# Routing to experts with unscaled transposes, token parts on VectorE, and the raw weight buffers at the top of SBUF

## The chip, the cores and the metric

The kernel runs on one core of a Trainium2 chip. The metric is device time in microseconds (us) for one execution. Five engines take part, each with its own instruction queue: the matrix engine (TensorE, in the profile PE, with PEld for its weight loads), VectorE (DVE), ScalarE (ACT), GpSimd (POOL) and SyncE (SP), which issues most transfers. They meet only at semaphores.

## The reference, cut to what matters

The program computes two transformer blocks on 256 tokens of width 1024. The first has a gated recurrence beside latent attention, cross-attention to a memory and a convolved feed-forward. The second has dilated and differential attention, a feed-forward, a gated recurrence in chunks (`hgrn`), and last a mixture of eight experts, of which each token uses two:

```
u = rms_norm(x, moe_norm)                 # x / rms(x) * gain, by token
logits = u @ w_router                     # 256 x 8
top_vals, top_idx = top_k(logits, 2)
top_w = softmax(top_vals)                 # over the two
gates = sum(one_hot(top_idx) * top_w)
for e in range(8):
    y = (silu(u @ w_gate[e]) * (u @ w_up[e])) @ w_down[e]
    out = out + gates[:, e:e+1] * y
x = x + out
```

All is fp32. The expert width is 3584. The row factor 1/rms(x) is one number for each token, so the logits of a token can be scaled by it after the product as well as before.

## The kernel before

**Weights.** All weights lie in memory as 458 pieces of 1 MB, called units (128 partitions x 2048 fp32); with three loaded again behind the last expert there are 461 loads. SyncE loads unit n into one of seven buffers of `raw`. ScalarE rounds it into one of three buffers of `wh` (`hi_to`, L1401, and `hi` in the expert loop, L2011), the high part. VectorE subtracts that from `raw` into `wl` (`lo_to`, L2087, and `lo`, L2990), the low part. The matrix engine makes each product from three: high x high, low x high, high x low (`split_product`, L421, L423, L430). A raw buffer is free for the next load when the low part is made; a `wh` buffer is free for the unit three later when its products are done. Units 0 to 121 (`N_FIXED` is 122) belong to everything ahead of the experts, and units 122 on to the experts, 42 each. The first three of the experts, 122 to 124, are prepared before the expert loop.

**Order.** The order of work on each engine is written out by hand. `hi_to(m)` and `lo_to(m)` say at which place in an engine's list units up to m are prepared. `step` makes VectorE wait for its own last operation.

**Normalisation.** There are two orders of it. For the names in `SCALED_LATER` the matrix engine transposes `x` as it is (L454), ScalarE and VectorE make high and low parts of the turned tiles with the gain (`norm_high`, L1434; `norm_low`, L2127), and the row factor comes in later. For the others, `moe_norm_2` among them, ScalarE squares both tiles (L1421), VectorE works out the factors and scales the rows into `xn` (L2103 to L2118), and then `xn` is transposed (L467). `residual` (L2150) adds the last projection's four PSUM banks to `x`.

**Routing, the seam.** After `residual` and the normalisation, the matrix engine makes the logits (8 x 256), VectorE copies them (L2912), the matrix engine turns them to token rows (L1211), and VectorE ranks them by comparing all pairs. L2918 and L2919 compare, L2922 multiplies ties by a fixed mask, one tile each, L2923 to L2925 add, reduce and compare with 2. Ten small matmuls (L441) count each token's slot in its expert, L2931 to L2938 turn that into slots, and `choose` (L2945) makes a 0/1 matrix `G` for the first expert.

Beside it, the tokens are split exactly into three bf16 parts, so that a matmul with `G` gathers them exactly. GpSimd multiplies the normalised rows by the gain (L2059, after the gain's transfer, L2055), ScalarE copies to bf16 (L1999, part 0), GpSimd subtracts (L2063), ScalarE copies (part 1), and VectorE subtracts into part 2 (L2952). The gather (L1234) has two runs of 24 matmuls, q = 0 for columns 0 to 511 and q = 1 for the others, and starts when all parts are there. ScalarE copies each run's bank (L2003) and VectorE subtracts (L2962); then the first expert's matmuls start. VectorE meanwhile clears `GT`, `yh` and `yl` (L2954 to L2957) and works out the two weights from an exponential (L2041; L2968 to L2983).

**Experts.** Fori loops on all engines, 42 units each, in chunks of 512 hidden columns. In the first chunk the matrix engine also scatters the previous expert's result (`scatter`, L1306 and L1307, which read `GT`, `yh` and `yl`), between the second and the third unit. For the first expert these hold zeros.

## Time and profile before

| what | before |
|---|---|
| median of 3 runs | 1944.0 us (1942.25 to 1947.37) |
| profiled execution, its own time | 1941.3 us |
| its span, first to last instruction | 1939.4 us |
| TensorE matmul busy | 1854.3 us (96%) |
| VectorE busy | 1552.2 us (80%) |
| ScalarE busy | 1255.3 us (65%) |
| GpSimd busy | 11.3 us (1%) |
| mean granted TensorE clock | 0.981 of 2.4 GHz |
| read from memory | 488.75 MB, 253 GB/s over the span |

The durations below come from the profiled execution, the comparison from the medians. A line such as L430 is a line of the kernel; a helper's line serves many callers. The granted clock is 1.00 at 2.4 GHz and 0.50 at 1.2 GHz. Idle time of an engine matters only where the chain that ended last runs through it.

### The profile page before, as it was taken

The page shows a single profiled execution, that of the slowest core. Times are in us where ns is not written, and L with a number is a line of the kernel's source. Part 1 is how long each engine was busy: PE and PEld are TensorE (multiplying, and loading weights), DVE is VectorE, ACT ScalarE, POOL GpSimd, SP SyncE. Part 2 cuts the span into 40 slices and gives each one's busy share as a digit, 9 for nine tenths or more (in the row PEclk, how much of TensorE's full clock was granted, in tenths as well). Part 3 has the DMA queues.
Part 4 walks back from the last instruction along what each step waited for, and adds up shares of the span by engine and source line. Part 5 has one row for each costly group of instructions (what it writes and reads, how often), then busy time and mean ns, then how long its engine had stood idle before and what let it go on. Part 6 is the DMA issues. An engine that isn't in the chain of part 4 may idle for free.

```text
span 1939.4 us, 27547 instructions
## 1 busy us (share of the span) xinstructions
PE 1854.3 (96%) x10240; PEld 1580.6 (82%) x10240; DVE 1552.2 (80%) x1589; ACT 1255.3 (65%) x1290; POOL 11.3 (1%) x9
## 2 busy tenths in 40 slices
PE   7888999998899999998799999999999999999997
PEld 7777999877799988876688888888888888888886
DVE  8966788476567645665898998989989899899997
ACT  6966565356554435554577777777777777777775
POOL 0000000000000000001000000000000000000000
PEclk9999999999799999999899999999999999999999
DMA  9422455542145554332499998999989989899894
GB/s 366 146 88 91 170 180 190 192 153 92 64 159 189 176 193 152 131 130 98 172 368 356 343 376 335 373 361 344 381 325 367 381 336 371 337 367 380 327 368 194
DMA packets 68330, 490.85 MB, mean 253 GB/s; under 512 B 7713, under 2 KB 8097, under 8 KB 8993
## 3 DMA queue, kind: packets, MB, share of 16 engines
q1 hardware_dynamic: 67968, 488.52, 67.1%
q0 software_dynamic: 288, 1.31, 0.2%
q8 instruction: 51, 0.84, 0.2%
q14 instruction: 23, 0.18, 0.0%
HBM read 488.75 MB, written 1.05 MB: 253 GB/s over the span
## 4 chain that ended last, share of the span: by engine, by line
PE 87%; DVE 6%; ACT 5%; issue 2%; DMA 0%; SPq 0%; ACTq 0%; DVEq 0%
PE ps L421 26%; PE ps L423 20%; PE ps L430 20%; PE ps L432 6%; PE ps L425 6%; DVE wl L2087 1%; PE ps L441 1%; PE ps L1322 1%; ACT wh L1401 1%; PE ps L1234 1%; PE ps L1053 1%; PE ps L467 1%; PE ps L1090 1%; PE ps L826 1%; PE ps L827 1%
## 5 line engine op out<-in xcount | busy, mean ns | idle before, releaser
L2990 DVE TENSOR_TENSOR wl<-raw,wh 128x2048 fp32r<-128x2048 f32 x336 | 761.1, 2288 | 63.3 <-ACT wh L2011 59.8
L2011 ACT ACTIVATE wh<-raw 128x2048 fp32r<-128x2048 f32 x336 | 642.1, 1918 | 180.9 <-PE ps L430 180.8
L421 PE MATMUL ps<-wh,hTh 128*128 128x512 f32 (+2 forms) x1128 | 443.2, 394 | 7.1 <-DVE hTl L2375 1.7
L2087 DVE TENSOR_TENSOR wl<-raw,wh 128x2048 fp32r<-128x2048 f32 x125 | 286.0, 2290 | 128.5 <-ACT wh L1401 127.9
L423 PE MATMUL ps<-wh,hTh 128*128 128x512 f32 x896 | 349.3, 390 | 0.0
L1401 ACT ACTIVATE wh<-raw 128x2048 fp32r<-128x2048 f32 x125 | 238.6, 1913 | 140.9 <-PE ps L430 73.2
L430 PE MATMUL ps<-wl,hTh 128*128 128x512 f32 (+2 forms) x1128 | 301.1, 386 | 0.0
L423 PE MATMUL ps<-wh,hTl 128*128 128x512 f32 (+2 forms) x680 | 260.4, 385 | 0.0
L421 PEld LDWEIGHTS ps<-wh,hTh 128*128 128x128 f32 x1128 | 212.2, 188 | 50.1 <-issue 5.4
L430 PEld LDWEIGHTS ps<-wl,hTh 128*128 128x128 f32 x1128 | 210.1, 188 | 42.8
L421 PE MATMUL ps<-hTh,wh 128*128 128x256 f32 x896 | 223.2, 286 | 2.5 <-DVE hTl L2127 2.3
L425 PE MATMUL ps<-hTl,wh 128*128 128x256 f32 x896 | 221.1, 284 | 0.0
L423 PEld LDWEIGHTS ps<-wh,hTh 128*128 128x128 f32 x896 | 168.4, 188 | 33.8
L421 PE MATMUL ps<-wh,hTl 128*128 128x512 f32 x448 | 176.9, 395 | 2.9 <-DVE hTl L2995 2.4
L421 PEld LDWEIGHTS ps<-hTh,wh 128*128 128x128 f32 x896 | 172.9, 193 | 4.9 <-issue 3.1
L425 PEld LDWEIGHTS ps<-hTl,wh 128*128 128x128 f32 x896 | 172.9, 193 | 0.1
L423 PEld LDWEIGHTS ps<-wh,hTl 128*128 128x128 f32 x680 | 128.2, 188 | 23.3
L430 PE MATMUL ps<-wl,hTl 128*128 128x512 f32 x448 | 138.1, 389 | 0.0
L432 PE MATMUL ps<-hTh,wl 128*128 128x256 f32 x896 | 125.7, 283 | 0.0
L432 PEld LDWEIGHTS ps<-hTh,wl 128*128 128x128 f32 x896 | 115.6, 192 | 0.0
L421 PEld LDWEIGHTS ps<-wh,hTl 128*128 128x128 f32 x448 | 84.1, 188 | 24.2 <-issue 7.5
L430 PEld LDWEIGHTS ps<-wl,hTl 128*128 128x128 f32 x448 | 84.1, 188 | 17.8
(433 smaller groups left out, 2026.4 us busy)
## 6 DMA issues: line engine op xcount, KB each, us to landing
raw<-in_units SPq DMA_DIRECT2D x461, 1024.0 KB, 6.9
x<-in_x SPq DMA_DIRECT2D x2, 512.0 KB, 5.4
work<-in_lru_w SPq DMA_DIRECT2D x1, 1024.0 KB, 15.4
xn<-in_mem SPq DMA_DIRECT2D x1, 1024.0 KB, 17.5
out<-x SPq DMA_DIRECT2D x2, 512.0 KB, 3.4
consts<-in_consts POOLq DMA_DIRECT2D x1, 768.0 KB, 4.6
work<-in_moe_gain POOLq DMA_DIRECT2D x1, 512.0 KB, 3.8
consts<-in_consts SPq DMA_DIRECT2D x1, 352.0 KB, 11.5
```

Source lines behind the costliest of these rows:

```text
L421: nc.tensor.matmul(out, sh, mh, start=(first and j == 0), stop=False)
L423: nc.tensor.matmul(out, sl, mh, start=False, stop=False)
L425: nc.tensor.matmul(out, sh, ml, start=False, stop=False)
L430: ins = nc.tensor.matmul(out, sh, ml, start=False, stop=done)
L432: ins = nc.tensor.matmul(out, sl, mh, start=False, stop=done)
L441: ins = nc.tensor.matmul(out, l, r, start=(first and j == 0), stop=(last and j == len(pairs) - 1))
L467: ins = nc.tensor.transpose(ps[:, NORM_BANK[name] + g, c2 * S + t * P:c2 * S + (t + 1) * P], rows_of(name)[:, t, c * P:(c + 1) * P], ident)
L826: nc.tensor.matmul(out, hTh[:, k, ts], hi[:, o], start=first, stop=False, skip_group_check=u == 2)
L1401: A(wh[:, n % SPLIT, :], raw[:, n % RAW, :], ACT.Copy).then_inc(sem("hi_made"), 1)
L2011: A(wh[:, n % SPLIT, :], raw[:, n % RAW, :], ACT.Copy).then_inc(sem("hi_made"), 1)
L2087: V.tensor_tensor(wl[:, n % SPLIT, :], raw[:, n % RAW, :], wh[:, n % SPLIT, :].bitcast(F32), ALU.subtract).then_inc(sem("lo_made"), 1)
L2990: V.tensor_tensor(wl[:, n % SPLIT, :], raw[:, n % RAW, :], wh[:, n % SPLIT, :].bitcast(F32), ALU.subtract).then_inc(sem("lo_made"), 1)
```

## The change

Four things are edited. The seven raw buffers move from the lowest addresses to above the work area, padded to a multiple of 128 bytes, and `work` and `junk` move with them; number and sizes are as before. `moe_norm_2` joins `SCALED_LATER`: `x` is turned unscaled, and the factor is applied to the logits when they are copied from PSUM. The tokens are scaled and split on VectorE, in halves of 512 columns (`tokens_half`, `tokens_rest`), with ScalarE's bf16 copies in halves between them (`token_part`), and GpSimd computes nothing. The second gather run waits for the second halves alone (`TOKEN_STEPS`). The two softmax weights come from two sigmoids in place of an exponential, an add, a reciprocal and a product. With them several things change place: the low part of unit 123 goes between the first two residual adds, that of unit 124 and the memsets go behind the gathered tokens' low parts, and the gain's transfer is issued once the previous mixer's outputs are turned, into `xn`, which is free then.

```diff
-    raw = sb("raw", [RAW, UNIT])
...
     xn = sb("xn", [TT, D])
-    junk = sb("junk", [HALF])
+    work_at = nc.sbuf_base
+    work = sb("work", [WORK])
     consts_at = nc.sbuf_base
     consts = sb("consts", [N_CONST])
     cols = sb("cols", [N_COLS])
     rows = sb("rows", [N_ROWS])
     pos = sb("pos", [TT], I32)
+    junk = sb("junk", [HALF])
     small = sb("small", [416])
-    work_at = nc.sbuf_base
-    work = sb("work", [WORK])
+    sb("pad", [(-nc.sbuf_base % 128) // 4])
+    raw = sb("raw", [RAW, UNIT])
 
...
-    moe_gain = area(4096, D)
+    moe_gain = xn[:, 0, :]
...
+    TOKEN_STEPS = (4, 6)
...
-    NORM_BANK = {n: 4 if n in ("hgrn_norm_2", "ffn_norm_2") else 0 for n in NORMS}
-    SCALED_LATER = ("mem_attn_norm", "attn_norm_2", "ffn_norm_2")
+    NORM_BANK = {n: 4 if n in ("hgrn_norm_2", "ffn_norm_2", "moe_norm_2") else 0 for n in NORMS}
+    SCALED_LATER = ("mem_attn_norm", "attn_norm_2", "ffn_norm_2", "moe_norm_2")
...
-        return area(0, TT, D) if name == "mem_attn_norm" else xn
+        return {"mem_attn_norm": area(0, TT, D), "moe_norm_2": area(10240, TT, D)}.get(name, xn)
...
-    rtv = {k: tiny(2) for k in ("v1", "v2", "ex", "w1", "w2")}
+    rtv = {k: tiny(2) for k in ("v1", "v2", "w1", "w2")}
...
         norm("moe_norm_2")
         pe.wait_ge(sem("router_lo"), 1)
-        split_product(ps[0:NE, 7, 0:S], [(rh[:, k * NE:(k + 1) * NE], rl[:, k * NE:(k + 1) * NE], hTh[:, k, :], hTl[:, k, :])
-                                         for k in range(KD)], ready=tile_ready, rest=lambda: None).then_inc(sem("logits"), 1)
+        for k in range(KD):
+            w = slice(k * NE, (k + 1) * NE)
+            tile_ready(k)
+            nc.tensor.matmul(ps[0:NE, 0, 0:S], rh[:, w], hTh[:, k, :], start=(k == 0), stop=False)
+            nc.tensor.matmul(ps[0:NE, 0, 0:S], rl[:, w], hTh[:, k, :], start=False, stop=False)
+            ins = nc.tensor.matmul(ps[0:NE, 0, 0:S], rh[:, w], hTl[:, k, :], start=False, stop=(k == KD - 1))
+        ins.then_inc(sem("logits"), 1)
         pe.wait_ge(sem("logits_read"), 1)
         for t in range(TT):
-            ins = nc.tensor.transpose(ps[:, 6, t * NE:(t + 1) * NE], logitsT[:, t * P:(t + 1) * P], ident[0:NE, 0:NE])
+            ins = nc.tensor.transpose(ps[:, 1, t * NE:(t + 1) * NE], logitsT[:, t * P:(t + 1) * P], ident[0:NE, 0:NE])
         ins.then_inc(sem("logits"), 1)
 
...
-                pe.wait_ge(sem("tokens_left"), 3)
+                pe.wait_ge(sem("tokens_left"), TOKEN_STEPS[q])
...
-        norm("moe_norm_2", N_FIXED + SPLIT)
-        for i in range(2):
-            act.wait_ge(sem("tokens_left"), i + 1)
-            A(parts[i][:], tokens[:], ACT.Copy).then_inc(sem("tokens_part"), 1)
+        A(warm, ones[:, 0:1], ACT.Sqrt)
+        norm_stats("moe_norm_2", (0,), False)
+        norm_high("moe_norm_2", 0)
+        norm_stats("moe_norm_2", (1,))
+
+        def token_part(i, h, left):
+
+            act.wait_ge(sem("tokens_left"), left)
+            cs = slice(h * HALF, (h + 1) * HALF)
+            A(parts[i][:, :, cs], tokens[:, :, cs], ACT.Copy).then_inc(sem("tokens_part"), 1)
+
+        token_part(0, 0, 1)
+        hi_to(N_FIXED + SPLIT)
+        token_part(1, 0, 2)
+        token_part(0, 1, 3)
+        token_part(1, 1, 5)
+        act.wait_ge(*reached("route_diff", 1))
+        A(rtv["w1"], rtv["v2"], ACT.Sigmoid, scale=-1.0)
+        A(rtv["w2"], rtv["v2"], ACT.Sigmoid).then_inc(sem("route_exp"), 1)
+
...
-        act.wait_ge(*reached("route_diff", 1))
-        A(rtv["ex"], rtv["v2"], ACT.Exp).then_inc(sem("route_exp"), 1)
...
-        pool.wait_ge(*reached("x_ready", X_AFTER["hgrn"]))
+        pool.wait_ge(*reached("hgrn_oT_ps", 4))
         pool.dma_start(moe_gain, moe_gain_d.partition_broadcast(P)).then_inc(sem("moe_gain"), 16)
-        pool.wait_ge(*reached("norm_xn", TT * len(NORMS)))
-        pool.wait_ge(sem("moe_gain"), 16)
-        for t in range(TT):
-            ins = G_.tensor_tensor(tokens[:, t, :], xn[:, t, :], moe_gain, ALU.mult)
-        ins.then_inc(sem("tokens_left"), 1)
-        pool.wait_ge(sem("tokens_part"), 1)
-        pool.wait_ge(sem("tokens_left"), 1)
-        G_.tensor_tensor(tokens[:], tokens[:], parts[0][:], ALU.subtract).then_inc(sem("tokens_left"), 1)
...
-        def residual(stage, n, following, bank=4):
+        def residual(stage, n, following, bank=4, then=0):
 
             lo_to(following + 1)
             for t in range(TT):
                 for h in range(2):
+                    if 2 * t + h == 1:
+                        lo_to(then)
...
-        residual("hgrn_x_change", 7, N_FIXED, 0)
-
-
-        norm("moe_norm_2", N_FIXED + SPLIT - 1)
+        residual("hgrn_x_change", 7, N_FIXED, 0, N_FIXED + 2)
+
+
+        norm_low("moe_norm_2", 0)
+        norm_rows("moe_norm_2")
+        token_scale = rstd[:, 2 * NORM_OF["moe_norm_2"]:2 * NORM_OF["moe_norm_2"] + TT]
+        dve.wait_ge(*reached("norm_xn", TT * len(NORMS)))
+        dve.wait_ge(sem("moe_gain"), 16)
+
+        def tokens_half(t, h):
+            cs = slice(h * HALF, (h + 1) * HALF)
+            return V.scalar_tensor_tensor(out=tokens[:, t, cs], in0=x[:, t, cs], scalar=token_scale[:, t:t + 1], in1=moe_gain[:, cs],
+                                          op0=ALU.mult, op1=ALU.mult)
+
+        def tokens_rest(i, h, part):
+
+            dve.wait_ge(sem("tokens_part"), part)
+            cs = slice(h * HALF, (h + 1) * HALF)
+            V.tensor_tensor((tokens, parts[2])[i][:, :, cs], tokens[:, :, cs], parts[i][:, :, cs],
+                            ALU.subtract).then_inc(sem("tokens_left"), 1)
+
         dve.wait_ge(sem("logits"), 1)
-        V.tensor_copy(logitsT, ps[0:NE, 7, 0:S]).then_inc(sem("logits_read"), 1)
+        V.tensor_copy(logitsT, ps[0:NE, 0, 0:S]).then_inc(sem("logits_read"), 1)
+        tokens_half(0, 0)
+        tokens_half(1, 0).then_inc(sem("tokens_left"), 1)
         L, rank, s1, s2, tmp = (rt[:, i] for i in range(5))
         dve.wait_ge(sem("logits"), 2)
-        step(V.tensor_copy(L, ps[:, 6, 0:TT * NE].rearrange("p (t e) -> p t e", t=TT)))
+        for t in range(TT):
+            ins = V.tensor_scalar(L[:, t, :], ps[:, 1, t * NE:(t + 1) * NE], token_scale[:, t:t + 1], None, ALU.mult)
+        step(ins)
...
-        lo_to(N_FIXED + SPLIT)
+        tokens_rest(0, 0, 1)
+        tokens_half(0, 1)
+        tokens_half(1, 1).then_inc(sem("tokens_left"), 1)
...
         choose(0)
-        dve.wait_ge(sem("tokens_part"), 2)
-        V.tensor_tensor(parts[2][:], tokens[:], parts[1][:], ALU.subtract).then_inc(sem("tokens_left"), 1)
-        dve.wait_ge(sem("tokens_left"), 3)
-        V.memset(GT.bitcast(F32), 0.0)
-        V.memset(gates[:, 0, :], 0.0)
-        V.memset(yh.bitcast(F32), 0.0).then_inc(sem("y_lo"), 1)
-        V.memset(yl.bitcast(F32), 0.0).then_inc(sem("y_lo"), 1)
-
...
-
-
+        tokens_rest(1, 0, 2)
+        tokens_rest(0, 1, 3)
         s1 = xsel
         for s, r, v in ((s1, 0.0, "v1"), (s2, 1.0, "v2")):
             step(V.tensor_scalar(s, rank, r, None, ALU.is_equal))
             step(V.tensor_tensor(tmp, s, L, ALU.mult))
             step(V.tensor_reduce(rtv[v], tmp, AX, ALU.add))
         V.tensor_tensor(rtv["v2"], rtv["v2"], rtv["v1"], ALU.subtract).then_inc(sem("route_diff"), 1)
+        tokens_rest(1, 1, 4)
+
...
+
+
         for q in range(2):
             tokens_low(q, 0)
+        lo_to(N_FIXED + SPLIT)
+        V.memset(GT.bitcast(F32), 0.0)
+        V.memset(gates[:, 0, :], 0.0)
+        V.memset(yh.bitcast(F32), 0.0).then_inc(sem("y_lo"), 1)
+        V.memset(yl.bitcast(F32), 0.0).then_inc(sem("y_lo"), 1)
         dve.wait_ge(*reached("route_exp", 1))
-        step(V.tensor_scalar(rtv["w1"], rtv["ex"], 1.0, None, ALU.add))
-        step(V.reciprocal(rtv["w1"], rtv["w1"]))
-        step(V.tensor_tensor(rtv["w2"], rtv["w1"], rtv["ex"], ALU.mult))
         for t in range(TT):
             step(V.tensor_scalar(tmp[:, t, :], s1[:, t, :], rtv["w1"][:, t:t + 1], None, ALU.mult))
             step(V.scalar_tensor_tensor(out=gates[:, 1:NE + 1, t], in0=s2[:, t, :], scalar=rtv["w2"][:, t:t + 1], in1=tmp[:, t, :],
```

## Rows read from the trace of the kernel before

**Rows 1.** The page, part 4: shares of the chain that ended last, by engine.
```profile
PE 87%; DVE 6%; ACT 5%; issue 2%; DMA 0%; SPq 0%; ACTq 0%; DVEq 0%
```

**Rows 2.** Windows by stage, under their own column heads.
```profile
core 0: us, PE busy (x) PEld busy (x) DVE busy (x) ACT busy (x) POOL busy (x), PEclk, DMA share, GB/s
907.00:939.00 32.00, 15.07 (x102) 13.08 (x100) 24.57 (x49) 12.45 (x17) 10.38 (x4) 0.68 0.23 83
...
1056.69:1179.97 123.28, 122.91 (x591) 101.58 (x591) 113.49 (x75) 91.85 (x64) 0.00 (x0) 1.00 0.94 358
```

**Rows 3.** Page part 5, the expert stage's high parts; waits of SyncE's queue (us, times, longest).
```profile
L2011 ACT ACTIVATE wh<-raw 128x2048 fp32r<-128x2048 f32 x336 | 642.1, 1918 | 180.9 <-PE ps L430 180.8
...
SPq L1345 <- DVE wl L2990: 781.5, 329, 18.0
```

**Rows 4.** Chain of waits through the seam: start us, us, what.
```profile
906.80 0.47 PE ps L430 x2
...
911.31 3.68 PE ps L467 x16
...
917.61 0.94 PE ps L430 x8
...
920.22 3.99 DVE work L2922
...
924.24 0.24 DVE work L2922
...
925.48 2.29 DVE wl L2087
...
930.06 2.21 DVE work_b L2952
...
932.41 5.02 PE ps L1234 x48
...
939.01 0.49 PE ps L421
```

**Rows 5.** Timeline at the `attn_norm_2` normalisation: start us, us, engine, line, what.
```profile
547.29 1.91 PE L454 MATMUL ps<-consts,x 128*128 128x128 f32 x16
...
549.45 3.23 DVE L2127 SCALAR_TENSOR_TENSOR hTl<-ps,cols,hTh 128x256 fp32r<-128x256 f32 x8 [1.27 <-ACT hTh L1434]
...
552.48 1.11 ACT L1421 ACTIVATE xn<-x 128x1024 f32<-128x1024 f32 x1
```

**Rows 6.** Page part 6 (KB, us to landing), then the seam's timeline.
```profile
work<-in_moe_gain POOLq DMA_DIRECT2D x1, 512.0 KB, 3.8
...
918.08 1.91 ACT L1999 ACTIVATE work_b<-work 128x2048 bf16<-128x2048 f32 x1 [0.41 <-POOL work L2059]
...
920.07 4.05 POOL L2063 TENSOR_TENSOR work<-work,work_b 128x2048 f32<-128x2048 f32 x1 [2.02 <-ACT work_b L1999]
...
938.07 1.28 ACT L2041 ACT_TABLE_LOAD   x1
```

**Rows 7.** Timeline of VectorE around the last residual adds and before.
```profile
891.19 1.23 DVE L2807 TENSOR_TENSOR xn<-xn,work 128x1024 f32<-128x1024 f32 x1
...
904.57 0.69 DVE L2150 TENSOR_TENSOR x<-ps,x 128x512 f32<-128x512 f32 x1 [0.67 <-PE ps L430]
...
909.84 1.42 DVE L2118 TENSOR_SCALAR xn<-x,small 128x1024 f32<-128x1024 f32 x2
```

**Rows 8.** Timeline of VectorE at the first expert's start.
```profile
934.73 0.11 DVE L2968 TENSOR_SCALAR work<-junk 128x16 f32<-128x16 f32 x1
...
941.26 0.38 DVE L2983 COPY junk<-junk 128x8 f32<-128x8 f32 x2
...
944.01 2.29 DVE L2990 TENSOR_TENSOR wl<-raw,wh 128x2048 fp32r<-128x2048 f32 x1 [2.37 <-ACT wh L2011]
```

**Rows 9.** Windows of 1 us through the seam, columns as in rows 2.
```profile
916.00:917.00 1.00, 1.00 (x9) 0.65 (x7) 0.77 (x2) 1.00 (x1) 1.00 (x1) 0.74 1.00 426
...
936.00:937.00 1.00, 1.00 (x12) 1.00 (x11) 0.67 (x2) 0.00 (x0) 0.00 (x0) 0.50 0.00 0
```

More of the change, by code:

```diff
@@ L2950, in _ @@
         choose(0)
-        dve.wait_ge(sem("tokens_part"), 2)
-        V.tensor_tensor(parts[2][:], tokens[:], parts[1][:], ALU.subtract).then_inc(sem("tokens_left"), 1)
-        dve.wait_ge(sem("tokens_left"), 3)
-        V.memset(GT.bitcast(F32), 0.0)
-        V.memset(gates[:, 0, :], 0.0)
-        V.memset(yh.bitcast(F32), 0.0).then_inc(sem("y_lo"), 1)
-        V.memset(yl.bitcast(F32), 0.0).then_inc(sem("y_lo"), 1)
-        def tokens_low(q, e):
-            dve.wait_ge(sem("tokens_hi"), e * 2 + q + 1)
-            V.tensor_tensor(xel[:, 4 * q:4 * q + 4, :], ps[:, TOKEN_BANKS[q], :].rearrange("p (a b) -> p a b", a=4),
-                            xeh[:, 4 * q:4 * q + 4, :].bitcast(F32), ALU.subtract).then_inc(sem("bank7_free"), 1)
+        tokens_rest(1, 0, 2)
+        tokens_rest(0, 1, 3)
         s1 = xsel
@@ L2971, in _, with tokens_low @@
         V.tensor_tensor(rtv["v2"], rtv["v2"], rtv["v1"], ALU.subtract).then_inc(sem("route_diff"), 1)
+        tokens_rest(1, 1, 4)
+        def tokens_low(q, e):
+            dve.wait_ge(sem("tokens_hi"), e * 2 + q + 1)
+            V.tensor_tensor(xel[:, 4 * q:4 * q + 4, :], ps[:, TOKEN_BANKS[q], :].rearrange("p (a b) -> p a b", a=4),
+                            xeh[:, 4 * q:4 * q + 4, :].bitcast(F32), ALU.subtract).then_inc(sem("bank7_free"), 1)
         for q in range(2):
             tokens_low(q, 0)
+        lo_to(N_FIXED + SPLIT)
[3 more added lines that the diff above has]
+        V.memset(yl.bitcast(F32), 0.0).then_inc(sem("y_lo"), 1)
         dve.wait_ge(*reached("route_exp", 1))
-        step(V.tensor_scalar(rtv["w1"], rtv["ex"], 1.0, None, ALU.add))
-        step(V.reciprocal(rtv["w1"], rtv["w1"]))
-        step(V.tensor_tensor(rtv["w2"], rtv["w1"], rtv["ex"], ALU.mult))
         for t in range(TT):
```

## The prediction

> **What bounds the kernel now.** I read the page first. The matrix engine carries 87% of the chain that ended last; VectorE has 6% of it, ScalarE 5% [rows 1]. That is an average over stages, so next come the windows by stage: the routing seam from 907 to 939 us, and the second expert [rows 2]. In an expert the matrix engine is busy for all but 0.4 us of 123.28 us; in the seam for 15 of 32 us. The feeding engines confirm it: of ScalarE's 180.9 us idle ahead of the 336 unit copies, the matrix engine ended 180.8, no transfer any, and SyncE's queue waits 781 us for buffers that VectorE frees [rows 3]. Nothing in the change touches an expert's matmuls. Hence an edit is worth what it takes from or adds to the time between the last projection matmul and the first expert matmul; whatever is left over then shifts the end one for one.
>
> The chain of waits through the seam [rows 4]: the last projection ends at 906.80 + 0.47 = 907.27, and the first expert matmul starts at 939.01. That is 31.7 us. Its marks are the end of the router product (917.61 + 0.94, logits read at 918.57), the gather's start (932.41) and its end (937.43). So there are three stretches: 11.3 us, 13.8 us and 6.6 us.
>
> **Stretch 1, to the logits.** Before, both tiles are summed and scaled before the transposes begin. Now `x` is transposed unscaled, the row factor is applied to the logits. The same order is in the trace for `attn_norm_2`: transposes start as the projection ends, at 547.29, and VectorE's eight low parts run from 549.45 to 552.68 [rows 5]. So 552.68 - 547.27 = 5.4 us from the last projection to the last low part. Then six router matmuls for the last pair of tiles, 0.12 us each at full clock as their 0.94 us for 8 show [rows 4], and a step of about 0.15: 6.3 us. Row statistics end earlier: the last square starts 552.48 - 547.27 = 5.2 us after the projections and takes 1.1 [rows 5], then come three tiny operations of 0.2. The saving is 11.3 - 6.3 = 5.0 us.
>
> The lower part of unit 123 (2.29 us [rows 4]) moves between the first and second residual add. Its cover is the projection still running, which lets an add start each 0.69 + 0.67 = 1.36 us [rows 7]. It makes the second add late (906.2 for 904.57), but the last three adds need 0.7 each and finish near 908.2; the transpose that needs the last one is thirteenth, at about 908.6. Without the cover it would cost up to 0.3. The gain vector's transfer moves forward, behind the turned outputs of the previous mixer; POOL's queue holds nothing else then, and it lands in 3.8 us [rows 6], more than 10 us before use.
>
> **Stretch 2, to the gather.** Start from 13.84 us and go in VectorE's order.
> - The tie product took 3.99 us once and 0.24 us for its twin [rows 4]. It ran beside GpSimd's subtraction of 4.05 us, from 920.07 to 924.12 [rows 6], and ended at 924.21. GpSimd now computes nothing: -3.75.
> - Two token halves before the logits are used, 128x512 with two inputs. VectorE's rows are 1.23 for 128x1024 with two inputs [rows 7] and 0.69 for 128x512 [rows 7]; back to back, 1.3 for two. They cover the wait for the small transposes, about 0.35: +0.95. Second scaling of the logits: +0.1.
> - Unit 124's low part leaves: -2.29.
> - The first remainder half comes in, +1.2, with two more token halves, +1.25. They cover the ten slot matmuls, which took no longer than unit 124's 2.29 us, since VectorE went on at its end (927.77) without a wait.
> - The last remainder before the gather shrinks from 2.21 us [rows 4] to a half, 1.2: -1.0.
> The sum is -3.75 + 0.95 + 0.1 - 2.29 + 1.2 + 1.25 - 1.0 = -3.55 us.
>
> ScalarE's copies to bf16 are now halves, about 1.06 each from 1.91 for the whole [rows 6]. The first ends about 1 us after the first two token halves, under VectorE's comparisons. Unit 124's high part (1.9 us) follows it, then each copy is ready before VectorE reaches its subtraction. If one were late, VectorE would stop for at most 1 us, and the slot steps, the routing of units and the gather queue behind it.
>
> For the token half no row has this operation with both inputs in SBUF. From below, the scaling of rows moves 128x1024 in 0.71 us [rows 7], so 0.36 a half; from above, 0.69. I take the upper, as two-input rows are all at that pace; four halves at the lower would give 1.3 us more.
> The Trainium skill (VectorE: DVE Perf Modes, "Mode 2×_2P — use both read ports for one tensor") says fp32 reaches two elements a cycle only with one tensor source. By it a two-source product runs at the slower pace, and the sum stays; were it wrong here, the sum would be 8.6 us.
>
> **Stretch 3, gather to expert.** The gather takes 5.02 us for 48 matmuls, then 1.6 us of copy, subtraction and start [rows 4]. Now the first half needs only the first halves of the parts. The second half waits for VectorE: a remainder (1.15), seven small routing steps (1.35 at the 0.2 us each that the ten slot operations and their handovers show between 927.77 and 930.06 [rows 4]), a second remainder (1.15), 0.1 of start. That is 3.75 us after the first start, where 24 matmuls take 2.5: +1.25 us. ScalarE's sigmoids, with a table load of 1.28 as its exponential had [rows 6], end before the second half does; the copy of the first half they delay is not the last thing needed. Their cover is gather work; uncovered they cost 1.7.
>
> Sum: 5.0 + 3.55 - 1.25 = 7.3 us less.
>
> **After the start.** Before, VectorE was free for the loop 2.6 us after the first expert matmul and then idle 2.37 us, so its first low part began at +5.0 [rows 8]. Now unit 124's low part (2.3), the memsets (2.3, from the gather's start to the first routing step at 934.73) and the gates (1.5, seven steps) stand behind the start: +6.0. The matrix engine needs unit 124's low part at +7.3 (two units of twelve matmuls and eight more, at the 0.23 that 0.47 for two gives [rows 4]) and has it at +2.2; it needs cleared `yh`, `yl` at +5.4 and has them at +4.4; it needs the loop's first low part after +11 and has it at +8.3. So nothing is priced, but the margin of 1.0 us at the scatter is the thinnest: every microsecond beyond it is paid in full.
>
> **Raw buffers at the top.** Same count, size and order of transfers. The same shapes cost the same on either side of the address range in this trace: whole-unit copies out of the lowest buffers and out of the area above them take 1.92 and 1.91 us [rows 3, 6]. No row has the loads at the top, so: zero, with a bound in the rivals.
>
> **The clock.** The granted clock was 0.50 through the old gather's first 4.6 us and rose only after it [rows 9]; an earlier stretch of work from 911.31 [rows 4] ran 5.2 us before the clock rose, within the window of 0.74 [rows 9]. The old gather is unbroken. The new one is two runs of 2.5 us with 1.25 us between and 1.6 us behind. My sum takes gathers at 1.2 GHz and experts at 2.4.
>
> **Rivals.**
> 1. The expert starts at 1.2 GHz. For it: the broken gather. Against: the total stretch is longer and the clock may rise inside it. Price: at most those 5.2 us at half pace, so 2.6 us, a saving of 4.7. Had the clock risen before the second half, that half would take 1.25: saving 8.5. [...]
> 2. Waits replace the stall: a part's copy late, or the scatter waiting for the memsets, 1 to 3.5 us together. For it: VectorE now does all the work that three engines shared. Against: every margin above but one exceeds 1 us. Saving 3.8 to 6.
> 3. The change doesn't remove the 3.99 us stall, because it came from the operation and not from GpSimd. Against: the twin of 0.24 and the common end. Saving 3.6.
> 4. Slower: loads into the top addresses take longer. In an expert the DMA engines are busy 0.94 of the time [rows 2], so from 6% longer transfers on they set the pace: 10% longer makes each of eight experts 123.28 x (0.94 x 1.10 - 1) = 4.2 us longer, 33 us in all, less the 7.3. For it only that the share is high; against it, in this trace SyncE waits for buffers and ScalarE for no transfer [rows 3], and no row ties a duration to an address.
>
> **How the numbers follow.** The profiled execution took 1941.3 us around a span of 1939.4; the median of the runs is 2.7 us above it. 1941.3 - 7.3 = 1934.0, and on the median 1944.0 - 7.3 = 1936.7 us. Chances: forecast (saving 6 to 8.8) 0.58; rival 1 0.20; rival 2 0.10; rival 3 0.03; rival 4 0.05; more than 8.8 saved 0.04. 0.3% of 1944 us, about what a measurement can tell from no change, is 5.8 us. The forecast and the larger saving give 0.62 faster, with 0.02 of rivals 1 and 2: 0.64. Their rest and rival 3 give 0.30 same, rival 4 and a miscount 0.06 slower. The range takes rivals 1 to 3 in and leaves rival 4 out. Its low end has the token halves at their lower price and the clock early, 7.3 + 1.3 + 1.25 = 9.9 us saved, 1934.1; its high end rival 3, 1940.4. The three runs' median lies 1.7 us above the lowest of them, so I add that on the low side and 1.1 on the high: 1932.5 to 1941.5.
>
> **What would show it.** In the profile after: logits read about 6.3 us after the last projection matmul; no VectorE product of 4 us; first gather about 10.3 us later; two gather runs with a gap; first expert matmul 24.4 us after the last projection; experts at 123.3 us each; an end 7 us earlier. Wrong if the clock column reads 0.50 behind the first expert matmul, if the matrix engine waits at the first scatter, or if an expert's length changes.

## The result, and the profile after

The changed kernel takes 1932.12 us (median of 5 runs, 1926.23 to 1932.88) where the kernel before takes 1945.72 us (median of 5, 1942.25 to 1950.11). The ratio is 0.992, with a 95% interval of 0.9902 to 0.9937: 12 to 19 us less. The forecast was 1936.7 us in a range of 1932.5 to 1941.5. The direction was right; the gain of 13.6 us is nearly twice the 7.3 us forecast, and the time is 0.4 us below the range.

The profiled execution took 1932.1 us around a span of 1930.3 us. The page of the changed kernel, its engine totals, the shares of the chain that ended last, the experts' high parts and the gain's transfer:

```profile
PE 1849.8 (96%) x10240; PEld 1582.5 (82%) x10240; DVE 1551.9 (80%) x1592; ACT 1236.9 (64%) x1277; POOL 1.4 (0%) x6
...
PE 87%; DVE 6%; ACT 5%; issue 2%; DMA 0%; SPq 0%; ACTq 0%; DVEq 0%
...
L2034 ACT ACTIVATE wh<-raw 128x2048 fp32r<-128x2048 f32 x336 | 644.0, 1919 | 198.7 <-PE ps L432 198.7
...
xn<-in_moe_gain POOLq DMA_DIRECT2D x1, 512.0 KB, 5.7
```

The chain reads as before [rows 1]. Three totals say more. GpSimd's 11.3 us are down to 1.4. ScalarE is busy 18.4 us less, which the forecast had no term for. Also TensorE's busy time is 4.5 us less, with the same 10240 matmuls; 2.0 of these lie in the windows of the seam (15.07 us in [rows 2], 13.07 below), the rest outside it. The gain's transfer takes 5.7 us, not 3.8 [rows 6], and still lands long before its use.

The chain of waits of the changed kernel through the seam (start us, us, what), to be read against [rows 4]:

```profile
907.73 0.46 PE ps L432 x2
908.19 1.11 PE ps L456 x10
...
914.46 0.41 DVE work L2944
914.87 1.32 DVE work L2933 x2
...
917.15 0.23 DVE work L2958
917.40 0.24 DVE work L2958
...
918.65 1.22 DVE work L2940
919.87 1.32 DVE work L2933 x2
...
923.05 1.13 DVE work_b L2940
924.18 1.14 DVE work L2940
...
926.63 1.15 DVE work_b L2940
927.91 2.73 PE ps L1241 x24
...
932.23 0.49 PE ps L423
```

L456 is now the transpose of unscaled `x`, L2933 a token half, L2940 a remainder half, L2958 the tie product, L1241 the gather. The last projection ends at 908.19, the first expert matmul starts at 932.23: 24.0 us for 31.7, against 24.4 forecast. The timeline of the matrix engine has both gather runs and what they waited for:

```profile
924.33 2.72 PE L1241 MATMUL ps<-work_b 128*128 128x128 bf16 x24 [3.43 <-DVE work_b L2940]
927.91 2.72 PE L1241 MATMUL ps<-work_b 128*128 128x128 bf16 x24 [0.87 <-DVE work_b L2940]
```

Windows of the changed kernel (columns as in rows 2): the seam, the end of the gather, and the second expert:

```profile
908.00:932.00 24.00, 13.07 (x101) 10.85 (x99) 18.17 (x51) 13.82 (x23) 0.00 (x0) 0.72 0.13 45
...
930.00:931.00 1.00, 0.63 (x6) 0.37 (x4) 0.00 (x0) 0.33 (x1) 0.00 (x0) 0.50 0.00 0
931.00:932.00 1.00, 0.00 (x0) 0.00 (x0) 0.70 (x2) 0.27 (x1) 0.00 (x0) 0.85 0.00 0
932.00:933.00 1.00, 0.77 (x3) 0.67 (x4) 1.00 (x1) 0.00 (x0) 0.00 (x0) 1.00 0.00 0
...
1049.71:1172.71 123.00, 122.67 (x590) 101.69 (x591) 113.63 (x75) 89.57 (x62) 0.00 (x0) 1.00 0.92 358
```

The clock is half through both gather runs and full when the expert starts. An expert takes 122.98 us from one scatter to the next (the mean of six distances, from the second scatter to the eighth) where it took 123.28. The first distance differs by 0.19 us only, and from the first scatter to the last, behind the eighth expert, it is 981.45 us for 983.73: 2.3 us less in all. The DMA share is 0.92 for 0.94 [rows 2], and the median unit lands 6.9 us after its issue in both, so the loads to the top addresses are no slower.

Two gains lie outside the seam. One is the table loads, in ScalarE's groups by form, of the kernel before, and neither of these two groups is there after:

```profile
L2011 ACT ACT_TABLE_LOAD x8 | 10.3, 1283 | 0.1
L2021 ACT ACT_TABLE_LOAD x8 | 10.3, 1283 | 6.9 <-PE ps L430 6.9
```

The other is the feed-forward's down product, 264 matmuls of 512 columns, which runs twice ahead of the seam. TensorE's groups by form between 325 and 420 us (count, then busy us and mean ns of one), of the kernel before and of the one after:

```profile
L423 PE MATMUL ps<-wh,work_r 128*128 128x512 f32 x88 | 35.0, 398 | 0.0
L421 PE MATMUL ps<-wh,work_r 128*128 128x512 f32 x88 | 34.6, 393 | 0.0
L430 PE MATMUL ps<-wl,work_r 128*128 128x512 f32 x88 | 27.6, 395 | 0.0
```

```profile
L425 PE MATMUL ps<-wh,work_r 128*128 128x512 f32 x88 | 34.2, 389 | 0.0
L423 PE MATMUL ps<-wh,work_r 128*128 128x512 f32 x88 | 34.2, 389 | 0.0
L432 PE MATMUL ps<-wl,work_r 128*128 128x512 f32 x88 | 27.1, 389 | 0.0
```

The busy times sum to 97.2 and 95.5 us: 1.7 us less, for the same matmuls with the same shapes. The start times say the same, 0.233 and 0.227 us from one matmul to the next, and so does the second stretch near 700 us. In the profile this doesn't bring the seam forward: its last projection ends 0.9 us later than before. The time at 1.2 GHz ahead of the seam is the same in both profiles, but four of its stretches fell in other places, at which the changed kernel falls back. Where they fall varies from profile to profile, so below the parts are sized by their own stretches and the whole by medians.

### The profile page after: what moved, and what is told of

Same layout as the page of the kernel before. It is cut to its first block, busy times and chain, and to the rows that moved or that the text cites. A ratio compares the mean times of both kernels' runs of the same rounds, so it can differ in the third digit from the quotient of the medians.

```text
span 1930.3 us, 27531 instructions
## 1 busy us (share of the span) xinstructions
PE 1849.8 (96%) x10240; PEld 1582.5 (82%) x10240; DVE 1551.9 (80%) x1592; ACT 1236.9 (64%) x1277; POOL 1.4 (0%) x6
## 4 chain that ended last, share of the span: by engine, by line
PE 87%; DVE 6%; ACT 5%; issue 2%; DMA 0%; SPq 0%; ACTq 0%; DVEq 0%
PE ps L423 26%; PE ps L425 20%; PE ps L432 20%; PE ps L434 6%; PE ps L427 6%; DVE wl L2100 1%; PE ps L443 1%; PE ps L1329 1%; ACT wh L1408 1%; PE ps L1241 1%; PE ps L1055 1%; DVE hTl L2140 1%; PE ps L1092 1%; PE ps L828 1%; PE ps L829 1%
## 5 line engine op out<-in xcount | busy, mean ns | idle before, releaser
L423 PE MATMUL ps<-wh,hTh 128*128 128x512 f32 (+2 forms) x1128 | 444.1, 395 | 6.8 <-DVE hTl L2390 1.7
L423 PEld LDWEIGHTS ps<-wh,hTh 128*128 128x128 f32 x1128 | 212.7, 189 | 50.3 <-issue 5.3
L423 PE MATMUL ps<-hTh,wh 128*128 128x256 f32 x896 | 225.6, 288 | 2.5 <-DVE hTl L2140 2.3
L423 PEld LDWEIGHTS ps<-hTh,wh 128*128 128x128 f32 x896 | 174.5, 195 | 5.4 <-issue 3.0
L423 PE MATMUL ps<-wh,hTl 128*128 128x512 f32 x448 | 176.0, 393 | 2.4 <-DVE hTl L3031 2.4
L423 PEld LDWEIGHTS ps<-wh,hTl 128*128 128x128 f32 x448 | 84.1, 188 | 20.8 <-issue 3.8
```

The lines of the kernel that those rows point to most:

```text
L423: nc.tensor.matmul(out, sh, mh, start=(first and j == 0), stop=False)
```

## The experiments

Three theories for the unforeseen 6 us were open: the table state at the entry of the expert loop, the addresses (of `raw`, or of `work`), and a larger saving at the seam than the profile shows. Of the seam, it was open whether GpSimd was what held VectorE. The kernel before ran beside each of them; the ratios are to those runs, with a 95% interval, and are not quotients of the medians in this table. e15, e16 and e18 ran once and stand for their profile's rows alone. "One expert" is the mean distance of scatters as above.

| kernel | median us (runs) | ratio | one expert, us | down matmuls, ns |
|---|---|---|---|---|
| after | 1932.12 (5) | 0.992 (0.9902 to 0.9937) | 122.98 | 389, 389, 389 |
| e4 after, old layout | 1938.47 (9) | 0.9957 (0.994 to 0.9973) | 122.92 | 398, 393, 396 |
| e3 before, new layout | 1939.87 (12) | 0.9974 (0.9963 to 0.9985) | 123.38 | 390, 390, 390 |
| e14 before, raw raised alone | 1945.34 (12) | 0.9996 (0.9983 to 1.001) | 123.28 | 398, 393, 395 |
| e13 before, work moved alone | 1941.86 (12) | 0.9981 (0.9967 to 0.9994) | 123.40 | 389, 389, 389 |
| e8 before, work 64 bytes up | 1943.74 (12) | 0.9993 (0.9981 to 1.0006) | 123.41 | 394, 394, 395 |
| e17 before, work 448 bytes up | 1939.91 (10) | 0.9979 (0.997 to 0.9989) | 123.36 | 389, 389, 389 |
| e18 before, work 192 bytes up | 1943.56 (1) | | 123.36 | 389, 389, 389 |
| e15 after, work 64 bytes up | 1932.29 (1) | | 123.10 | 398, 393, 395 |
| e16 after, work 128 bytes up | 1933.38 (1) | | 123.03 | 394, 394, 395 |
| e1 before, sigmoids | 1939.84 (12) | 0.9984 (0.9971 to 0.9998) | 122.92 | |
| e2 before, table alone | 1943.62 (12) | 0.9986 (0.9973 to 0.9998) | 122.92 | |
| e5 after, exponential | 1934.71 (5) | 0.9942 (0.9923 to 0.9962) | 123.39 | |
| e11 before, tokens on VectorE | 1944.97 (10) | 1.0004 (0.9993 to 1.0015) | 123.28 | |
| e7 after, GpSimd busy | 1936.44 (5) | 0.9956 (0.9939 to 0.9973) | 122.98 | |
| e6 after, gather in one | 1932.72 (4) | 0.9931 (0.9911 to 0.9951) | 122.98 | |
| e12 after, junk moved too | 1928.96 (6) | 0.9919 (0.9902 to 0.9936) | 122.95 | |

**The layout, undone and done alone.** e4 is the changed kernel with the old order of buffers, e3 the old kernel with the new order (the change's first hunk).

> The changed kernel with the old addresses (raw lowest, work above the constants). Table theory: the same time as the changed kernel, ratio 0.992, experts 122.98 us, seam 24.1 us. Rival (addresses matter): 2.4 to 8 us slower than the changed kernel, ratio 0.993 to 0.996.

> The kernel before with only the addresses changed: raw buffers above the others. Table theory: nothing, seam 31.7 us, experts 123.28 us, ratio 1.000. Rival (addresses matter): experts shorter by 0.3 us each or the stages ahead of the seam shorter, 2.4 to 8 us less.

Both runs say that the layout is worth something, e3 by 5.1 us (2.9 to 7.2). In e3 the seam is 31.9 us as before; what got shorter is the down product, and in e4 it is as long as before. So the step "Raw buffers at the top: zero" is wrong in its number.

**Which address.** e14 moves `raw` up and leaves `work` at its address; e13 leaves `raw` at the bottom and moves `work` down.

```diff
 e14: -    raw = sb("raw", [RAW, UNIT])
      ...
           xn = sb("xn", [TT, D])
      +    raw = sb("raw", [RAW, UNIT])
 e13:      xn = sb("xn", [TT, D])
      -    junk = sb("junk", [HALF])
      +    work_at = nc.sbuf_base
      +    work = sb("work", [WORK])
      ...
      +    junk = sb("junk", [HALF])
      ...
      -    work_at = nc.sbuf_base
      -    work = sb("work", [WORK])
```

> The kernel before with the raw buffers moved up over wh, wl, x and the turned tiles, to between xn and junk; the work area keeps its address. Address theory: the matmuls on the hidden parts stay at 395 to 400 ns, ratio 1.000. Rival (raw below the weights' buffers is the cause): 389 to 393 ns, 3.5 us gained, ratio 0.998.

> The kernel before with the work area moved down, to just above xn (constants, junk and small above it), the raw buffers still lowest: work starts at about 156 thousand bytes from the bottom in place of 173 thousand. Address theory (the feed-forward down products cost more when the hidden parts they read lie near the top): matmuls on them between 389 and 395 ns, faster for the first parts than for the last. Rival (they cost more when the raw buffers lie below the weights' buffers, whatever the work area's place): 395 to 400 ns as before.

`raw`'s place costs nothing (398, 393 and 395 ns stay). The place of `work`, which holds the down product's moving operand, does it all. The slope from the first parts to the last that I expected of e13 isn't there: all three lines take 389 ns. What of that place? `work` begins 98880 bytes above `wh` before, 64 more than a multiple of 256, and 81920 after, a multiple of 256. Five kernels pad `work`:

```diff
 e8:  +    sb("pad", [(-nc.sbuf_base % 128) // 4])   # 64 bytes; distance 98944
 e17: +    sb("pad", [112])                          # 448 bytes; distance 99328
 e18: +    sb("pad", [48])                           # 192 bytes; distance 99072
 e15: +    sb("off", [16])                           # after, 64 bytes; e16: [32], 128 bytes
           work_at = nc.sbuf_base
           work = sb("work", [WORK])
 e15: +    sb("rest", [16])                          # behind it the same; e16: [32]
```

> The kernel before with one pad of 64 bytes ahead of the work area, so that it starts at a multiple of 128 bytes as in the changed kernel; the raw buffers stay lowest. Start theory (the matmuls of the two feed-forward down products read their 512-column operand from the work area, and cost 395 ns where they cost 389 when it starts at 64 bytes past a multiple of 128): those matmuls at 389 ns, the two stretches 1.7 us shorter each, ratio 0.998 as with all addresses changed. Rival (it is the raw buffers' place that counts): 395 ns and ratio 1.000.

> The kernel before with 448 bytes of pad ahead of the work area, so that it starts a multiple of 1024 bytes above the weights' buffers and still near the top. Offset theory: 389 ns, 3.5 us gained, ratio 0.998. Height theory: 394 to 398 ns, ratio 1.000.

> The kernel before with 192 bytes of pad ahead of the work area: a multiple of 256 bytes above the weights' buffers, near the top. Offset theory: 389 to 394 ns, less than the 394 of a multiple of 128 alone. Height theory: 394 to 398 ns.

> The changed kernel with work and everything above it moved up by 64 bytes, near the bottom still. Offset theory (the matmuls on the hidden parts depend on the work area's start relative to the weights' buffers, not on how high it lies): 395 to 398 ns as before. Height theory (only an area near the top is slow): 389 ns.

> The changed kernel with the work area alone moved up by 128 bytes. Offset theory: about 394 ns, as in the run with the work area at a multiple of 128 bytes near the top. Height theory: 389 ns.

The same groups as above, of e8:

```profile
L422 PE MATMUL ps<-wh,work_r 128*128 128x512 f32 x88 | 34.7, 394 | 0.0
L424 PE MATMUL ps<-wh,work_r 128*128 128x512 f32 x88 | 34.7, 394 | 0.0
L431 PE MATMUL ps<-wl,work_r 128*128 128x512 f32 x88 | 27.6, 395 | 0.0
```

and of e17, of which the other two take 389 ns as well:

```profile
L425 PE MATMUL ps<-wh,work_r 128*128 128x512 f32 x88 | 34.2, 389 | 0.0
...
```

I had expected 64 bytes more to be enough, since that makes the start a multiple of 128; it brings 0.3 of the 1.7 us (from the first of a stretch's 264 matmuls to the last, by their starts, it is 61.11 us for 61.37, and 59.64 in e17). At distances from `wh` that are multiples of 256 bytes (after, e3, e13, e17, e18) a matmul takes 389 or 390 ns, at 128 off (e8, e16) 394, at 64 off (before, e4, e14, e15) 398, 393 and 395, whether `work` lies high or low. e17 brings 4.1 us of time (2.1 to 5.8) for 448 bytes of padding, about the 3.5 us of two stretches. Whether the distance between the two operands counts, or each operand's start by itself, isn't told apart: `raw`, which moves from below `wh` to above it, is itself a multiple of 256 bytes long, so `wh` starts at the same remainder in every run. The reason within the matrix engine isn't known. The Trainium skill (SBUF — State Buffer, "SBUF: two separate sides") says that the matrix engine never waits on another engine's use of SBUF; by it the difference, up to 2.3% with the address alone, isn't a wait for another engine. No run here tests that. The same kernels have an expert 0.08 to 0.13 us longer than their partners (e3, e8, e13, e17 and e18, 123.36 to 123.41 for 123.28); in e15 and e16, at 64 and 128 off, it is longer than in the changed kernel too (123.10 and 123.03 for 122.98). So that is a second effect of the layout that doesn't follow the multiples of 256, and its cause is open.

**The table state.** The sigmoid of the weights is the last function ahead of the loop in the changed kernel, and the sigmoid is the loop's only function beside its copies. e1 puts it into the old kernel, e2 keeps the exponential and only runs an unused sigmoid behind it, e5 puts the exponential back.

```diff
 e1: -        A(rtv["ex"], rtv["v2"], ACT.Exp).then_inc(sem("route_exp"), 1)
     +        A(rtv["w1"], rtv["v2"], ACT.Sigmoid, scale=-1.0)
     +        A(rtv["ex"], rtv["v2"], ACT.Sigmoid).then_inc(sem("route_exp"), 1)
 e2:          A(rtv["ex"], rtv["v2"], ACT.Exp).then_inc(sem("route_exp"), 1)
     +        A(warm, ones[:, 0:1], ACT.Sigmoid)
 e5: -        A(rtv["w1"], rtv["v2"], ACT.Sigmoid, scale=-1.0)
     -        A(rtv["w2"], rtv["v2"], ACT.Sigmoid).then_inc(sem("route_exp"), 1)
     +        A(rtv["ex"], rtv["v2"], ACT.Exp).then_inc(sem("route_exp"), 1)
```

> The kernel before with only the two sigmoids in place of the exponential, add, reciprocal and product. Table theory (the exponential leaves another activation table in place at the expert loop's entry, so each of eight iterations loads two tables of 1.28 us, and VectorE's late chain then holds the first down product by about 0.3 us): no table load at the loop's copies or sigmoids, experts of 122.98 us in place of 123.28, 2.4 us less in all, the seam as before at 31.7 us. Rival (the experts got shorter because the raw buffers moved): experts stay at 123.28 us and the time stays.

> The kernel before, exponential kept, with one more ScalarE instruction behind it: a sigmoid of a constant column. Table theory: the same as with the two sigmoids, experts at 122.98 us, 2.4 us less, table loads in the loop gone, because only the table that stands at the loop's entry counts. Rival (fewer VectorE steps at the start or the raw placement shorten the experts): experts stay at 123.28 us.

> The changed kernel with the exponential and its three VectorE steps back. Table theory: two table loads of 1.28 us in each expert iteration again, experts 0.3 to 0.4 us longer than 122.98, so 2.4 to 3 us in all; the seam as in the changed kernel. Rival (the sigmoids' table load alone matters, once): experts stay at 122.98 us.

e1 and e2 have no table load in the loop and 122.92 us for an expert; e5 has them again, in ScalarE's groups by form:

```profile
L2033 ACT ACT_TABLE_LOAD x8 | 10.3, 1283 | 0.1
L2043 ACT ACT_TABLE_LOAD x8 | 10.3, 1283 | 6.9 <-PE ps L432 6.9
```

with 123.39 us for an expert. So one state at the loop's entry decides sixteen loads: 0.36 us an expert in the old layout and 0.41 in the new, 2.7 and 3.4 us from the first scatter to the last. e2 does it with one operation more and no sigmoid in the arithmetic; the ratios of e1 and e2 are worth 3.1 us (0.4 to 5.6) and 2.7 us (0.4 to 5.3). How the load reaches the matrix engine is in the second expert's first down product. The timelines of ScalarE, VectorE and the matrix engine before:

```profile
1188.66 1.28 ACT L2011 ACT_TABLE_LOAD   x1
...
1198.58 1.28 ACT L2021 ACT_TABLE_LOAD   x1 [0.86 <-PE ps L430]
...
1191.90 4.49 DVE L2990 TENSOR_TENSOR wl<-raw,wh 128x2048 fp32r<-128x2048 f32 x2 [0.94 <-ACT wh L2011]
...
1209.08 0.68 DVE L2995 TENSOR_TENSOR hTl<-ps,hTl 128x512 fp32r<-128x512 f32 x1
...
1208.76 1.07 PE L430 MATMUL ps<-wl,hTh 128*128 128x512 f32 x4
1209.89 0.49 PE L421 MATMUL ps<-wh,hTl 128*128 128x512 f32 x1
```

and of VectorE and the matrix engine after:

```profile
1181.40 6.76 DVE L3026 TENSOR_TENSOR wl<-raw,wh 128x2048 fp32r<-128x2048 f32 x3 [0.20 <-ACT wh L2034]
...
1200.84 0.68 DVE L3031 TENSOR_TENSOR hTl<-ps,hTl 128x512 fp32r<-128x512 f32 x1
...
1201.44 1.07 PE L432 MATMUL ps<-wl,hTh 128*128 128x512 f32 x4
1202.34 0.39 PE L423 MATMUL ps<-wh,hTl 128*128 128x512 f32 x1
```

Before, the load of 1188.66 stands ahead of ScalarE's next copy into `wh`, and VectorE waits 0.94 us for that copy in the middle of its low parts; after, three of them run with no wait between. VectorE then has no idle time in which to make it up ahead of the hidden tile. Before, its low part of that tile begins 0.32 us after the four matmuls that need none of it, the next product starts 1.13 us after their first one (1209.89 - 1208.76) and its first matmul takes 0.49. After, the low part begins 0.60 us ahead of them, and the product follows at 0.90 with 0.39. e2, which is the kernel before with one operation more, has the times of the kernel after: the low part 0.64 us ahead, the product at 0.90 with 0.39. So of the two loads of 1.28 us on ScalarE all but this third of a microsecond was covered here. The price of one load, 1283 ns, is what the Trainium skill gives (ScalarE: Activation LUTs, "What ACT_TABLE_LOAD costs"); most of it lies under other work here.

**GpSimd and VectorE.** e7 gives the changed kernel a GpSimd subtraction of 128x2048 on unused space, as the logits are turned. e11 gives the old kernel GpSimd's products and subtraction to VectorE, at the same places in its order and in whole tiles.

```diff
 e7:  +        pool.wait_ge(sem("logits"), 2)
      +        spare = area(8192, 2048)
      +        G_.tensor_tensor(spare, spare, spare, ALU.subtract)
 e11: -            ins = G_.tensor_tensor(tokens[:, t, :], xn[:, t, :], moe_gain, ALU.mult)
      -        G_.tensor_tensor(tokens[:], tokens[:], parts[0][:], ALU.subtract).then_inc(sem("tokens_left"), 1)
      +            ins = V.tensor_tensor(tokens[:, t, :], xn[:, t, :], moe_gain, ALU.mult)
      +        V.tensor_tensor(tokens[:], tokens[:], parts[0][:], ALU.subtract).then_inc(sem("tokens_left"), 1)
```

> The changed kernel with one GpSimd subtraction of 128x2048 added (an area against itself, its result unused), started when the small transposes of the logits are done, so beside the comparisons and tie products. Port theory: a two-input VectorE operation inside its 4 us takes up to 4 us, the seam grows by 3 to 4 us. Rival (the stall had another cause): the small operations stay at 0.24 to 0.30 us and the seam at 24.1 us.

> The kernel before with GpSimd's two token products and its subtraction done by VectorE, whole and in the places they had (the products behind the low parts, the subtraction behind the selection). Port theory (the 3.99 us tie product waited for GpSimd's subtraction beside it): both tie products near 0.24 us, 3.75 us gained, but 2.4 us of products and 2.3 us of subtraction come into VectorE's list; the seam ends at 31 to 33 us, so about nothing. Rival (the product itself is slow): one tie product stays near 4 us and the seam grows to about 36 us.

The timeline of e7:

```profile
911.92 4.36 POOL L2079 TENSOR_TENSOR work<-work 128x2048 f32<-128x2048 f32 x1 [18.66 <-PE ps L1218]
...
913.12 3.31 DVE L2957 TENSOR_TENSOR work<-junk 128x128 f32<-128x128 f32 x1
916.46 0.29 DVE L2958 TENSOR_TENSOR work<-junk 128x128 f32<-128x128 f32 x1
```

GpSimd ends at 916.28 and the comparison at 916.43; its twin, the same operation on the other tile, takes 0.29. The seam is 27.06 us for 24.04, 3.02 more, which is also what the comparison takes above its twin. This profile also shows rival 1. In its windows at the first expert's start (931.86) the granted clock is still half:

```profile
933.00:934.00 1.00, 1.00 (x4) 0.81 (x3) 1.00 (x2) 0.00 (x0) 0.00 (x0) 0.50 0.00 0
934.00:935.00 1.00, 1.00 (x4) 0.77 (x4) 0.84 (x3) 0.00 (x0) 0.00 (x0) 0.62 0.27 33
```

From 931.86 to the rise at 934.8 the expert runs 2.9 us at half pace, and from its first matmul to the end it takes 999.54 us where the changed kernel's profile takes 998.07: 1.5 us more. e11 is the other way about. Its chain of waits:

```profile
924.97 0.24 DVE work L2919
925.23 0.24 DVE work L2919
...
926.47 2.29 DVE work L2925
...
935.16 4.31 PE ps L1234 x48
```

The tie product takes 0.24 both times, and the same subtraction that took GpSimd 4.05 us takes VectorE 2.29. The 3.99 us were GpSimd's work, not the operation's. e11's seam is 29.4 us, 2.3 less than before; 0.7 of these are the clock, which rose earlier in its gather (4.31 us for 5.02). The time doesn't show the other 1.6 (the ratio is 1.0004, and even the low end of its interval is 1.4 us less); where they went is open.

**The split gather.** e6 lets both runs of the gather wait for all parts, as before.

```diff
-    TOKEN_STEPS = (4, 6)
+    TOKEN_STEPS = (6, 6)
```

> The changed kernel with both gather runs waiting for all halves of the parts. If the split is worth what the profile shows: the first run starts 3.6 us later, both run back to back in 5.0 us at half clock, the first expert matmul comes 1.2 us later (seam 25.7 us for 24.0). If the clock rises within the unbroken gather, up to 1.2 us of that comes back.

The seam is 25.68 us (907.07 to 932.75), 1.6 us more, though the clock rose within its gather; by the ratios it can't be told from the changed kernel.

**A version that might beat both.** e12 also moves `junk` from above `pos` to beside `work`, so that more starts are round.

```diff
     xn = sb("xn", [TT, D])
+    junk = sb("junk", [HALF])
     work_at = nc.sbuf_base
```

> The changed kernel with junk moved down beside the work area, so that it starts at a multiple of 128 bytes too, raw still on top. If junk's place is what made experts 122.98 us here and 122.92 us with the old addresses, experts fall to 122.92 us, 0.5 us in all; otherwise nothing changes. Ratio to the kernel before 0.992.

It has the lowest median, 1928.96 us, but the ratio's interval lies over that of the changed kernel, and an expert is 122.95 for 122.98, half of what I expected of `junk`'s place. Its profile has one lesson, in the windows around the start of the second gather run, at 923.01:

```profile
922.00:923.00 1.00, 0.14 (x2) 0.02 (x1) 0.86 (x1) 0.99 (x3) 0.00 (x0) 0.60 0.00 0
923.00:924.00 1.00, 0.99 (x18) 1.00 (x19) 0.38 (x1) 0.59 (x3) 0.00 (x0) 1.00 0.06 16
```

Here the clock rose before the second run, which took 1.51 us for 2.73, and the seam is 22.9 us. In e15 and e16 it did so too. In e6 it rose within the unbroken gather, in e4 and e5 between gather and expert, in e7 behind the expert's start. So between near variants of one program the seam and what follows differ by some 2.7 us with the clock alone (1.2 less in e12's seam, 1.5 more behind e7's).

## Why the prediction was right and wrong

**The seam: right, by its steps.** Stretch 1, from the last projection to the logits: 11.3 to 6.3 us was forecast, 914.46 - 908.19 = 6.27 measured. One argument for it doesn't hold: the row statistics were said to end earlier, but the prediction's own figures for them add to 5.2 + 1.1 + 0.6 = 6.9 us, and VectorE makes the row factor ahead of its copy of the logits. They were in time (the factor at 914.09) because the change puts the first tile's square ahead of the high parts, so that the last square starts 4.0 us after the last projection and not 5.2; that the 6.3 came out is in part luck. Stretch 2, to the gather: 10.3 forecast, 924.33 - 914.46 = 9.87 measured. The removed stall is as costed (0.23 and 0.24 for the tie products, and e7 brings it back), two token halves take 1.32 for 1.3, so the pace taken for two inputs was right, a remainder half 1.13 to 1.22 for 1.15 to 1.2; what makes up the 0.4 left isn't worked out. Stretch 3, to the expert: 7.85 forecast, 932.23 - 924.33 = 7.90 measured, with the second run 3.58 us behind the first for 3.75. In all 7.7 us saved for 7.3, in the one profile that was taken.

**After the start: the margins held, the experts' length didn't.** The first scatter starts 5.43 us after the first expert matmul in both kernels, so the cleared `yh`, `yl` and unit 124 cost nothing there. But from the first expert matmul to the end the time is 998.07 us for 1000.39, and these 2.3 us are the experts' own, which the prediction had named as a sign that it was wrong.

**The step that failed: "Nothing in the change touches an expert's matmuls. Hence an edit is worth what it takes from or adds to the time between the last projection matmul and the first expert matmul."** Two edits reach beyond it.
1. The sigmoids were costed once, where they stand, with a table load as the exponential had. They change the state in which the loop is entered. Sixteen table loads of 1283 ns stood in the loop before, in ScalarE's groups, and I had looked at the busiest group only. Worth 0.36 to 0.41 us an expert (e1, e2, e5). The layout takes 0.06 of it back in each (122.98 us for e4's 122.92), which leaves the 0.30, and 2.3 us in all.
2. **"Raw buffers at the top: zero"**, because "no row ties a duration to an address". Rows of the kernel before did: of the down product's matmuls those of L423 took 398 ns and those of L430 395, where the same lines with the same shape take 389 to 390 in the experts. (L421's 393 didn't show it, since there it takes 394 to 395.) I priced the part of the edit that has the name, `raw`, which is indeed worth nothing (e14), and not the `work` that moves with it (e13, e17): 1.7 us in each of two stretches, 3.5 us.

The sum is 7.7 + 2.3 + 3.5 = 13.5 us, inside the 12 to 19 us of the interval. That it meets the 13.6 between the medians to 0.1 is luck, with stretches of the clock that fall otherwise from run to run. e4 and e3 part the whole, but more coarsely: without the layout the ratio is worth 8.4 us (5.3 to 11.7), where the parts give 10.5 (7.7 and the 2.8 of e4's experts); the layout alone 5.1 us (2.9 to 7.2), where the 3.5 less the 0.7 that it adds to e3's experts give 2.8, at the edge of that interval.

**The rivals.** Rival 1, the expert at 1.2 GHz, didn't happen in the profile of the changed kernel, where the clock was half through the whole gather and rose 0.9 us ahead of the expert. It did happen in e7, for 1.5 us of the 2.6 that I gave as its most; and the early rise, which I gave no chance beyond 0.04, came in four variants (e6, e12, e15, e16). So all three cases occur. How often each does in the changed kernel's unprofiled runs isn't known, so the third theory, a larger saving at the seam than its profile shows, is neither shown nor ruled out; no run holds the clock fixed, and its rule isn't settled here. The Trainium skill (TensorE: Matmul & The Clock Gate, "HAM oscillation — how this bites in real kernels") tells of a kernel whose waits for transfers between short bursts of matmuls let the clock fall before each burst. No run here shows that: the clock stood at half ahead of the first gather run already, and with 0.87 us of waiting between the runs it stayed there in the changed kernel and rose in that gap in e12. Rival 2: each remainder ran back to back with what stood ahead of it, and no wait took the stall's place. Rival 3 falls by e7 and e11. Rival 4 falls: the experts' DMA share went from 0.94 to 0.92, a unit lands 6.9 us after its issue in both, and SyncE's longest wait for an expert's low part from 18.0 to 5.6 us [rows 3]:

```profile
SPq L1352 <- DVE wl L3026: 766.0, 329, 5.6
```

## What to carry to other kernels

Cost a change of function tables by the state that it leaves for the next loop, not only where it stands: group ScalarE's loads by form and ask for each what ran before it on the first pass and on each later one. When a buffer moves, find who reads every buffer that moves with it, and compare the mean of one matmul, line by line, between stages with the same shape; where it differs, pad an operand to a multiple of 256 bytes from the other and look again. And keep GpSimd off tensors in SBUF while VectorE has a short chain with two inputs from SBUF.

## What the hardware showed that was not expected

- A 512-column fp32 matmul takes 389 or 390 ns with its moving operand's buffer a multiple of 256 bytes from the weights' buffer, 394 at 128 off, and 393 to 398 at 64 off, that is 0.227 us (256) or 0.233 us (64) from one to the next. Height in SBUF doesn't matter (99328 and 81920 bytes apart are alike).
- Table loads in a loop body stood in each of eight passes or in none, by the state at its entry: the code placed ahead of the loop decides them. An unused sigmoid of one column ahead of it removes sixteen.
- One GpSimd operation of 4.36 us held a VectorE operation of 0.29 us with two inputs from SBUF for 3.31 us, to its own end; VectorE's reads from PSUM beside it went on (0.34 us for two).
